# Retention's values by seven products of half tiles, and six of the eight rotations moved to the gates' slots

## What is computed

```python
z = jnp.einsum('bsd,dc->bsc', x, w_in) + b_in
q_a, k_a, v_a, q_r, k_r, v_r, g_r, gate_a, gate_b = jnp.split(z, SPLIT_POINTS, axis=-1)
...
y_r = _retention(q_r.reshape(B, S, RET_HEADS, RET_QK_DIM),
                 k_r.reshape(B, S, RET_HEADS, RET_QK_DIM),
                 v_r.reshape(B, S, RET_HEADS, RET_V_DIM))
y_b = (jax.nn.silu(g_r) * y_r.reshape(B, S, RET_V_WIDTH)).astype(x.dtype)
merged = (jax.nn.sigmoid(gate_a) * jnp.einsum('bsc,cd->bsd', y_a, w_attn_proj)
          + jax.nn.sigmoid(gate_b) * jnp.einsum('bsc,cd->bsd', y_b, w_ret_proj))
...
def rot(t):
    t1, t2 = t[..., :half], t[..., half:]
    return jnp.concatenate([t1 * cos - t2 * sin, t1 * sin + t2 * cos], axis=-1).astype(t.dtype)
```

## Time and profile before

| | us |
|---|---|
| median of 3 runs | 3385.14 (3383.45 to 3390.64) |
| the profiled execution | 3385.06 |
| its span | 3382.9 |
| outside the span | 2.2 |

### The profile page before, as it was taken

How to read it: one execution, slowest core, us unless ns; L and a number is a source line. 1 busy time by engine, 2 the same in 40 slices (tenths; PEclk the granted TensorE clock), 3 DMA queues, 4 the chain that set the end, 5 groups by cost and what they waited for, 6 DMA issues and landing times.

```text
span 3382.9 us, 61672 instructions
## 1 busy us (share of the span) xinstructions
PE 3257.3 (96%) x26818; PEld 2766.2 (82%) x26818; DVE 1880.3 (56%) x3603; ACT 526.8 (16%) x1035; POOL 876.4 (26%) x710
## 2 busy tenths in 40 slices
PE   7999999789999899999999999999999999999999
PEld 3444445478888799999889999899899998998998
DVE  5533544376666267476547657455177465561673
ACT  2000001133333111110121011122010102120111
POOL 1000100022121067676116610000066200000564
PEclk9999999999999799999999999999999999999999
DMA  8555763100000044445415565333445443334453
GB/s 340 189 199 179 264 216 110 66 6 6 6 7 6 15 149 164 160 170 171 162 65 173 191 216 188 113 125 131 149 138 175 170 162 113 125 102 166 137 167 121
DMA packets 69787, 466.22 MB, mean 138 GB/s; under 512 B 7360, under 2 KB 10048, under 8 KB 16793
## 3 DMA queue, kind: packets, MB, share of 16 engines
q1 hardware_dynamic: 52272, 368.07, 31.8%
q0 software_dynamic: 12192, 87.04, 6.9%
q10 hardware_dynamic: 5065, 7.27, 0.7%
HBM read 456.59 MB, written 5.77 MB: 137 GB/s over the span
## 4 chain that ended last, share of the span: by engine, by line
PE 90%; DVE 7%; ACT 2%; issue 1%; DMA 0%; POOL 0%; DVEq 0%; ACTq 0%; POOLq 0%
PE ps L760 30%; PE ps L654 22%; PE ps L1170 14%; PE ps L800 3%; PE ps L1180 3%; PE ps L846 1%; PE ps L833 1%; PE ps L852 1%; PE ps L1199 1%; PE ps L1254 1%; PE ps L1115 1%; PE ps L1229 1%; PE ps L893 1%; PE ps L946 1%; PE ps L919 1%
## 5 line engine op out<-in xcount | busy, mean ns | idle before, releaser
L603 POOL TENSOR_TENSOR arena<-ring 128x512 f32<-128x512 f32 (+1 forms) x170 | 233.0, 1370 | 1464.9 <-DMA ring<-in_w_fx_gu 1013.9
L760 PE MATMUL ps<-arena 128*128 128x128 f32 x4400 | 521.7, 275 | 4.4 <-DVE arena L1703 2.6
L760 PEld LDWEIGHTS ps<-arena 128*128 128x128 f32 x4400 | 505.7, 192 | 6.3 <-DVE arena L1703 3.5
L654 PE MATMUL ps<-y,ring 128*128 128x512 f32 (+1 forms) x1408 | 462.6, 491 | 9.9 <-DVE y L2112 4.2
L654 PEld LDWEIGHTS ps<-y,ring 128*128 128x128 f32 x1408 | 270.4, 192 | 200.1 <-issue 170.2
L760 PE MATMUL ps<-arena,ring 128*128 128x128 f32 x2200 | 275.3, 275 | 0.8 <-issue 0.8
L654 PE MATMUL ps<-arena,ring 128*128 128x256 f32 (+1 forms) x864 | 263.1, 466 | 1.4 <-DVE arena L1870 1.4
L760 PEld LDWEIGHTS ps<-arena,ring 128*128 128x128 f32 x2200 | 261.0, 192 | 1.5 <-issue 1.0
L609 POOL TENSOR_TENSOR arena<-ring,arena 128x512 f32<-128x512 f32 (+1 forms) x170 | 251.2, 1478 | 13.3
L1689 DVE TENSOR_TENSOR arena<-ring 128x512 f32<-128x512 f32 (+1 forms) x170 | 201.0, 1187 | 92.7 <-DMA ring<-in_w_f_down 49.0
L654 PEld LDWEIGHTS ps<-arena,ring 128*128 128x128 f32 x864 | 164.1, 190 | 99.2 <-issue 83.7
(11 more groups left out here) (352 smaller groups left out, 4885.3 us busy)
## 6 DMA issues: line engine op xcount, KB each, us to landing
ring<-in_w_f_gu SPq DMA_DIRECT2D x88, 1024.0 KB, 4.9
arena<-in_ada_t POOLq DMA_DIRECT2D x72, 1024.0 KB, 5.3
ring<-in_w_fx_gu SPq DMA_DIRECT2D x44, 1024.0 KB, 4.9
ring<-in_w_f_down SPq DMA_DIRECT2D x36, 1024.0 KB, 4.9
ring<-in_w_fx_down SPq DMA_DIRECT2D x24, 1024.0 KB, 4.9
ring<-in_w_qk_a SPq DMA_DIRECT2D x18, 1024.0 KB, 5.0
ring<-in_w_qk_r SPq DMA_DIRECT2D x16, 1024.0 KB, 4.9
ring<-in_w_v_r SPq DMA_DIRECT2D x16, 1024.0 KB, 4.9
```

The costliest lines, as they stand in the source:

```text
L603: nc.gpsimd.tensor_tensor(both, quarter(s, 2, n), quarter(s, 3, n), ALU.add) \
L654: last = mm(out, w, rhs_, start=(k == 0 and s.opens), stop=(k == kts - 1 and s.closes))
L760: last = mm(out, weights[number][:, j * P:(j + 1) * P], inputs[number](base + j), start=(s.opens and j == 0 and number in (1, 5)), stop=(s ...
```

## The change

`v_r` is cut into quarters too, and takes `projected` and `projection_out` in place of `half_tokens` and L2328. It uses the form of `v_a`: activations stationary, weights moving, bias along a row; its bias steps (`ret_steps`) are made once a layer, beside `row_steps`. The evictions of `qk_r`'s last two slots, which had no sums ahead, now carry those for `v_r`'s first two slots. Rotation 0 and 4 stay in the first loop, at halves 27 and 29; rotations 1, 5, 2, 6, 3, 7 go to halves 1, 3, 7, 9, 13, 15 of the second, into two scratch tiles of their own (`late_rot_a`, `late_rot_b`, in space that the attention's values have left). Everything is done for both layers. The arithmetic of the other stages and the count and size of the transfers stay.

```diff
-               (f"qk_r{_l}", 8, 1, "quarters_cols", "w_in_2", _l, 3456), (f"v_r{_l}", 8, 1, "cols", "w_in_2", _l, 5504),
+               (f"qk_r{_l}", 8, 1, "quarters_cols", "w_in_2", _l, 3456), (f"v_r{_l}", 8, 1, "quarters_cols", "w_in_2", _l, 5504),
...
-        PROJECTIONS = {"qk_a": (0, 0), "v_a": (9, None), "qk_r": (14, 18), "g_r": (22, 34), "gate": (30, 50)}
+        PROJECTIONS = {"qk_a": (0, 0), "v_a": (9, None), "qk_r": (14, 18), "v_r": (22, None), "g_r": (30, 34), "gate": (38, 50)}
...
-        early_sums, early_quads, row_steps = take(2, 4, 512), take(2, 4, P), take(5, P)
+        early_sums, early_quads, row_steps, ret_steps = take(2, 4, 512), take(2, 4, P), take(5, P), take(8, P)
         cursor[0] = 0
         late_sums, late_quads = take(2, 4, 512), take(2, 4, P)
+        late_rot_a, late_rot_b = take(2, SEQ), take(2, SEQ)
...
-                            last = mm(quarters_bank(s)[:, REGION[number]], *((x, w) if base == "v_a" else (w, x)),
+                            last = mm(quarters_bank(s)[:, REGION[number]], *((x, w) if base in ("v_a", "v_r") else (w, x)),
                                       start=(j == 0 and number in (1, 5)), stop=(j == 3), skip_group_check=True)
...
-                def half_tokens(s, name, m):
-                    if m == 0:
-                        pe.wait_ge(landed[s.pos], landed_by(name, s))
-                        pe.wait_ge(psum_free, s.group + 1)
-                    for k in range(KD):
-                        last = mm(ps[:, 2 * s.par, m * SEQ:(m + 1) * SEQ], h1(k)[:, m * P:(m + 1) * P],
-                                  ring[:, s.pos, k * 256:(k + 1) * 256], start=(k == 0), stop=(k == KD - 1))
-                    if m == 1:
-                        last.then_inc(slots_used, 1)
...
-                    if i < 16:
-                        projected(s, name, HALF[i % 2])
-                    else:
-                        half_tokens(s, name, i % 2)
+                    projected(s, name, HALF[i % 2])
...
-                if base == "v_a":
+                if base in ("v_a", "v_r"):
                     at = 256 * s.l
-                    lo, hi, second = v_a[:, 0, at:at + P], v_a[:, 1, at:at + P], v_a[:, :, at + P:at + 2 * P]
+                    values, row, steps = (v_a, at, row_steps) if base == "v_a" else (v_r, 1280 + at, ret_steps)
+                    lo, hi, second = values[:, 0, at:at + P], values[:, 1, at:at + P], values[:, :, at + P:at + 2 * P]
                     v.wait_ge(slots_used, s.n + 1)
-                    tt(quad[:, 3], bank[:, 0], brow[:, at:at + P], ALU.add).then_inc(*step(f"dve.{s.key}_one"))
+                    tt(quad[:, 3], bank[:, 0], brow[:, row:row + P], ALU.add).then_inc(*step(f"dve.{s.key}_one"))
...
-                    tt(quad[:, 1], quad[:, 1], row_steps[:, s.l], ALU.add).then_inc(*step(f"dve.{s.key}_four"))
+                    tt(quad[:, 1], quad[:, 1], steps[:, s.l], ALU.add).then_inc(*step(f"dve.{s.key}_four"))
...
-                        tt(row_steps, rows[:, :, 1], rows[:, :, 0], ALU.subtract).then_inc(*step(f"dve.row_steps{l}"))
+                        tt(row_steps, rows[:, :, 1], rows[:, :, 0], ALU.subtract)
+                        rows = brow[:, 1280:3328].rearrange("p (n m t) -> p n m t", n=8, m=2)
+                        tt(ret_steps, rows[:, :, 1], rows[:, :, 0], ALU.subtract).then_inc(*step(f"dve.row_steps{l}"))
...
                 def rotate(n):
...
-                    if n:
-                        v.wait_ge(*past(f"dve.rot{l}_{n - 1}"))
-                    else:
+                    rot_a, rot_b = first_rot if n % 4 == 0 else (late_rot_a, late_rot_b)
+                    if n == 0:
                         v.wait_ge(psum_free, released(f"v_r{l}"))
+                    elif n != 1:
+                        v.wait_ge(*past(f"dve.rot{l}_{n - 4 if n > 3 else n + 3}"))
...
-                    if i % 2 and i < 16:
+                    if i % 2:
                         n = 14 + i // 2
-                        projection_out(*todo[n], todo[n + 2] if n + 2 < 22 else None)
-                    elif i % 2:
-                        s = v_r_slots[i // 2 - 8]
-                        v.wait_ge(slots_used, s.n + 1)
-                        row = brow[:, 1280 + 256 * s.l:1536 + 256 * s.l]
-                        both = ps[:, 2 * s.par, :].rearrange("p (m t) -> p m t", m=2)
-                        tt(v_r[:, :, 256 * s.l:256 * s.l + 256], both, row.unsqueeze(1).to_broadcast([P, 2, 256]),
-                           ALU.add).then_inc(psum_free, 1)
-                        rotate(i // 2 - 8)
-                        if i == 29:
+                        projection_out(*todo[n], todo[n + 2] if n + 2 < 30 else None)
+                        if i == 27:
+                            rotate(0)
+                        elif i == 29:
+                            rotate(4)
                             v.wait_ge(*past(f"pe.ya{l}_{len(QT) - 1}"))
                         if i >= 29:
-                            whole_sum(*todo[22 + (i - 29) // 2])
+                            whole_sum(*todo[30 + (i - 29) // 2])
...
                     if i % 2:
-                        n = 22 + i // 2
-                        projection_out(*todo[n], todo[n + 2] if n + 2 < 38 else None)
+                        n = 30 + i // 2
+                        projection_out(*todo[n], todo[n + 2] if n + 2 < 46 else None)
+                    if i in (1, 3, 7, 9, 13, 15):
+                        rotate(i // 6 + 1 + (0 if i % 6 == 1 else 4))
```

6 lines of the change are left out of this document (3 added, 3 removed).

## The result

| | before | after |
|---|---|---|
| median of 6 runs each, measured together | 3385.35 (3383.45 to 3390.64) | 3374.68 (3367.57 to 3377.36) |
| the profiled execution | 3385.06 | 3374.66 |
| its span | 3382.9 | 3372.4 |

The ratio after to before is 0.9960, with a 95% interval of 0.9948 to 0.9972: 0.4% faster. On the scale of the 3385.14 us shown at first that ratio is 3371.6 us. The forecast was 3374.3. The after executions' own median is 0.4 us from it, but by the ratio the time is 0.6 us under the low end of my range, 3372.2. The quotient of the two medians is 0.9968, which is 3374.5 us on that scale; the ratio on record lies 0.0008 under it, inside its interval.

What follows compares the result with a forecast made beforehand. PE was taken to bound the kernel, busy 96% of the span and all of `v_r`. 3385.06 less 10.8 us saved on PE, with DVE's added work costing nothing, gave 3374.3 us; range 3372.2 to 3378.5.

Steps and rivals of the forecast that it cites:

- The term of the sum: PE in `v_r`: seven products for eight save 0.655 us a slot with full attention, 0.70 otherwise; 10.8 us for both layers.
- DVE in `v_r`: DVE's work in the `v_r` stage rises from 31.25 to 45.3 us of some 65.7, without making PE wait.
- the retention stage: Six rotations moved here add 12 us of DVE work beside 90.22 busy in 163.10, at no cost.
- The seam and the mean's subtraction: DVE deadlines at half 29, before `g_r`, and in the retention stage: room 1.1 and 1.5 us, cost nothing.
- Rival (a): Part given back at the seam or at `v_r`'s transposes waiting for DVE: 3376 to 3379 us; chance 0.08.
- Rival (c): Retention stage: moved rotations miss the deadline at the mean's subtraction, PE stops and the kernel is slower; chance 0.03.
- p = 3.85 us: Cost of one moved rotation, in place of 2.00 us, from which PE's stops reach 10.8 us and the kernel is slower.
- The rule on the weight loads: Skill's rule that weight loads' busy share is the good measure; in `v_r`, 59.53 of 71.10 us, it put the gain in doubt.
- the width of the range: Whole kernel's time: 3372.2 to 3378.5 us, the forecast itself given 0.84 within about 0.7 us each way.

Runs made afterwards that it cites:

- before_keep: Kernel before the change, plus idle PE products in the tail of the first block's scan: 3378.99 us, ratio 0.9986 to the kernel before.
- keep_clock: Changed kernel, plus idle PE products in the tail of the first block's scan: 3368.82 us, ratio 0.9951 to the kernel before.
- values_only: Changed kernel with its seven products in `v_r`, but all rotations back at their old places: 3376.17 us, ratio 0.9966 to the kernel before.
- late_8: Changed kernel with eight extra DVE operations ahead of the subtraction of the mean at each of heads 0 to 2, both layers: 3409.67 us.
- seam_5: Changed kernel with five extra DVE operations at half 29, ahead of the sums for the first `g_r` slot, both layers: 3384.39 us.
- seam_3: Changed kernel with three extra DVE operations at half 29, ahead of the sums for the first `g_r` slot, both layers: 3377.39 us.
- after_again: Changed kernel, unedited, measured again: 3374.84 us, ratio 0.9965 to the kernel before.

## Why the prediction was right, and where it failed

- **The term of the sum.** 0.70 us a slot without attention and 0.655 with, 5.4 a layer, 10.8 in all: measured 5.25 and 5.25 in the traces, 10.5 between before_keep and keep_clock at `g_r`, 10.8 over all executions. The mechanism is right and the term a little too large. A pair of slots with attention is 2163.54 - 2144.75 = 18.79 us, to 0.01 what `qk_r` had told. The two pairs with little or nothing between them, priced at 1.40, gained 1.31 each as well (from 16.97 us to 15.66, and from 13.92 to 12.61, where 12.5 was reckoned), so the 4 x 0.70 = 2.80 measured 2.62. What came is the term's own lower bound, 16 x 0.655 = 10.5.
- **What was luck.** That the profiled execution, 3374.66, lies 0.4 us from the forecast is in part chance: the 10.5 us had 1.06 us added to them ahead of the change and 1.1 taken away in fx_1, and neither was in the sum. That all executions together give exactly 10.8 is chance too, with two standard errors of 1.6.
- **DVE in `v_r`.** 45.3 us reckoned, 46.9 measured; the retention stage 12 more reckoned, 11.3 measured. The sum took six rotations out of the stage, but its window loses five (seven in it before, two after): the eighth already ran behind its end. values_only, with seven in the window, shows what five are worth, 56.58 - 46.88 = 9.7 us. The sum also left out the sums for `v_r`'s second slot, which fall into the window; the rest was not followed further, since DVE has the room.
- **The seam and the mean's subtraction.** Room 1.1 and 1.5 us reckoned, 1.25 and 1.62 measured, and late_8, seam_5 and seam_3 show that they are the deadlines.
- **Rival (a), part given back.** In none of its places: PE waits nowhere in `v_r` or at the seam. The 1.1 us in fx_1, 270 us behind the last changed stage, come from a meeting of DVE with POOL, and it is not shown that the change has a part in it.
- **Rival (c), slower by late rotations.** Its mechanism is real (late_8), and its price was too low. I priced a stop of PE at its own length. The stops of late_8 cost 32.3 us for 20.5, so the point from which the change would have been slower lies earlier than the p = 3.85 us I gave.
- **The rule on the weight loads.** The loads rose from 59.5 of 71.1 us to 62.5 of 65.8 and never held PE: the row had it right, not the rule.
- **The step that failed is the width of the range, at its low end.** The chances put the time "within about 0.7 us each way" of the forecast, and the low end was "3385.1 - 11.2 less the 1.7 us by which the lowest run shown lies under its median": the ends of the term and three executions of before gave the spread. The unchanged kernel after runs from 3367.6 to 3381.3 in 19 executions, and before from 3378.5 to 3391.4 in 82. A median of 6 from such a spread (3.2 us) is uncertain by some 1.6 us (1.25 x 3.2 / √6, one standard error), and the three ratios measured, 0.9960, 0.9965 and 0.9973, put one and the same change at 3371.6, 3373.3 and 3376.0 on the scale of 3385.14. The set of the result is the lowest of the three, and has the fastest of all 19 executions in it (3367.57, at a mean clock of 0.992). All executions together put it at 3385.14 x 3375.16 / 3385.96 = 3374.3 us. The clock rows for this were in the profile before: the span's mean clock of 0.989 says that some stretches run at the lower level; that they fall differently in other executions of the same program only the later traces showed. I had asked for the clock only in the stage that changes.

## What to carry to other kernels

Price a form of product from a stage that already has it, with the same neighbours: the pair of `qk_r` slots gave the new pair of `v_r` slots to 0.01 us. Before work is moved to make room, run the change without the move: the rotations fitted in their old places, with 0.15 us of DVE's idle time and 1.5 us ahead of PE. Before a wait found in one trace is laid to the change, look for the same wait in a stage that the change does not touch. And take the range's width from how executions differ (the clock of stages far from the change), not from the spread of three of them.

## What the runs showed of the hardware

- A stop of PE can cost more than its length. Behind stops of 2.84 to 3.71 us eight records took up to 3.78 us in place of 1.89, in five cases of six clearly, and 20.5 us of such stops cost 32.3. Of three stops of 2.14 and 2.15 us two were followed by the lower clock (seam_5 once, after_again); behind 0.70 us it did not come (seam_3, twice).
- Idle products in a stage that leaves PE pausing keep the granted clock up (0.92 for 0.55), and brought 5.9 us without any other change.
- A DVE operation of 128x128 with two SBUF inputs takes 0.28 us, or up to 1.39 when an operation of POOL's sum has begun just before it, and whether it has is decided by the arrival of a transfer, within 0.4 us.
